# Output projections as stages of their own, a head-group loop turned by half, and gain work inside the FFN loop of a decoder layer

## Chip, core and metric

The kernel runs on one core of a Trainium2 chip. The metric is the device time of one execution in microseconds. TensorE is called PE in the rows, VectorE DVE, ScalarE ACT, GpSimd POOL, SyncE SP; SP issues nearly all DMAs.

## What is computed

One decoder layer for 256 tokens of width 2048 in float32. The part that matters, cut from the reference:

```python
mod = jax.nn.silu(c) @ w_ada[l] + b_ada[l]            # 2048 x 12288, six pieces of 2048
sh_m, sc_m, ga_m, sh_f, sc_f, ga_f = jnp.split(mod[:, None, :], N_MOD, axis=-1)
h = rmsnorm(x, g_pre_mix[l]) * (1.0 + sc_m) + sh_m
# token mixer, 16 heads of 128
hq, hf, hi, hg, cq, ckv, kr, gate_a, gate_b = jnp.split(h @ w_in, split_idx, axis=-1)
o = hgrn2_chunked(q, k, v, log_f)                     # gated recurrence per head
o = rmsnorm(o, g_hg_out) * jax.nn.silu(hg)
y_a = o.reshape(B, S, HG_VWIDTH) @ w_o_hg             # output projection 1, 2048 x 2048
att = causal_block_attention(q_full, k_full, v_m)     # latent attention per head
y_b = att.reshape(B, S, MLA_HEADS * V_DIM) @ w_o_mla  # output projection 2, 2048 x 2048
merged = jax.nn.sigmoid(gate_a) * y_a + jax.nn.sigmoid(gate_b) * y_b
y = merged @ w_out
x = x + ga_m * rmsnorm(y, g_post_mix[l])
h = rmsnorm(x, g_pre_ffn[l]) * (1.0 + sc_f) + sh_f
y = swiglu(h, w_gate_up[l], w_down[l])                # 2048 -> 5632 -> 2048
return x + ga_f * rmsnorm(y, g_post_ffn[l])
```

## The kernel before

**Chunks.** All weights come in chunks of 256 rows by 512 columns (512 KB), 600 in all, through a ring of 4 slots. SP loads a chunk into `raw` (`load`) once VectorE is done with the slot. ScalarE rounds it into `whi` (`high`, line 374) once TensorE is done with the slot's last chunk. VectorE subtracts, `wlo = raw - whi` (`low`, line 1001). TensorE does 12 matmuls with it (`multiply`, lines 707 to 709): 2 token tiles x 2 row blocks x 3 products of high and low halves. So each engine's program is one list of chunks, in the same order, with its other work written by hand between them. ScalarE and VectorE can be three chunks ahead of TensorE and no more: VectorE reaches chunk c while TensorE is near c - 3. Each projection of 512 columns adds up in one of two pairs of PSUM banks; the pair is free for the next but one when somebody has read it (`pair_free`). Four more banks, XA and XB, serve transposes, scores and sums.

**Stages.** Start (80 chunks): input norm, compressed queries and keys, the gates; then a loop over 4 groups of 4 heads with 56 chunks each; `w_out` (32); the FFN as a loop over 11 blocks of 512 (264).

**A group (c = 0 to 55).** Chunks 0 to 7: queries, keys, rotary queries (two chunks of half width), values of the attention; 8 to 23: forget gate and query of the recurrence, beside which the attention runs (scores at 11, softmax, sums at 19); 24 to 39: value and output gate of the recurrence, beside which it runs: logarithms and `k` on ScalarE, 8 scans on VectorE behind `low(27)` (line 1264), `q_ready` behind 29 (line 1269), then eight decay levels at `DECAY` = c 31, 32, 34, ... 41. For a level GpSimd forms differences (`differences`, lines 192, 193), ScalarE exponentials, VectorE two products (`decay`, lines 1283, 1284), TensorE scores (line 896), VectorE a masked merge (line 1297). TensorE does the self scores (line 882) and those of the first level behind chunk 29. The output gate is made at c = 42 and 43 (lines 1318, 1321), the sum over keys behind c = 41, the norm at c = 45 (lines 1326 to 1335). Chunks 40 to 47: the group's part of `w_o_mla`; 48 to 55: its part of `w_o_hg`, 2 chunks per 512 columns. Each of these 8 products of a group is multiplied by its gate (line 1352) and added to `merged` (line 1357) on VectorE. Behind the loop `merged` is transposed (`transpose_merged`) and split for `w_out`.

**Modulation.** `mod` is a product of one row, so VectorE does it: `ada_acc += slot * csilu` (line 1008), one operation per 512 KB load. The first 64 loads belong to the start; the others, 128, go at one per chunk at c = 3 to 18 and 24 to 39 of each group (`ada_chunk`), through two slots of `ada_raw`; SP issues a load when the operation two before is done. TensorE sums the partitions (`sum_rows`, line 742, 8 matmuls per sum). The gains behind the two post norms are spread over the partitions with diagonals (`make_gain`, `spread_gain`, lines 1365 and 927), both in the `w_out` stage.

A program-level float32 matmul of the small kind counts as two instructions in the trace; a transpose as one.

## Time and profile before

| | |
|---|---|
| median of 3 runs | 1981.98 us (1979.76 to 1985.1) |
| profiled execution | 1982.95 us, its span 1981.0 us |
| busy TensorE, VectorE, ScalarE, GpSimd | 1859.5, 1375.7, 885.5, 138.9 us |
| first, second, third, fourth group | 200.3, 206.6, 202.1, 203.7 us |
| `w_out` stage, FFN from its second chunks to the last block | 100.8, 714.0 us |
| DMA, mean | 213 GB/s |

A busy time counts instructions in execution; those of TensorE overlap their neighbours, so its waits are best seen as idle time in front of an instruction. The releaser named behind it is the last to come of those that it waited for. "issue" as a releaser means that the profile shows none. The granted clock is a share of the full one.

### The profile page before, as it was taken

Reading aid. Unit: us, or ns where it says so; the run is one execution under the profiler, and the core shown is the slowest. Engines: PE = TensorE matmul, PEld = TensorE weight load, DVE = VectorE, ACT = ScalarE, POOL = GpSimd, SP = SyncE. Lnnn points to the kernel's source line nnn. Section 1 sums busy time; section 2 is a strip of 40 time slices with the busy share of each in tenths; the row PEclk is TensorE's granted clock in tenths of the full one; section 3 lists DMA queues with packets and bytes.
Section 4 is the critical chain, followed back from the end, with each engine's and each line's share of the span. In section 5 each row is a group of like instructions: output and inputs, shape, how many; then the busy total and the mean of one; then the engine's idle time right before and its main releaser. Section 6 shows DMA issues by size and latency. Waiting matters only on the chain. (4 is left out here: it accounts for less than half of the span.)

```text
span 1981.0 us, 25357 instructions
## 1 busy us (share of the span) xinstructions
PE 1859.5 (94%) x8940; PEld 1554.0 (78%) x8940; DVE 1375.7 (69%) x1336; ACT 885.5 (45%) x985; POOL 138.9 (7%) x76
## 2 busy tenths in 40 slices
PE   1999999999899999899989996999999999999995
PEld 1877888788787878787878885788888888888884
DVE  5799767789769876987698755556555655565555
ACT  4544455643463436444644443444434444444442
POOL 0000000140014000500050000000000000000000
PEclk9999999999999999999999998999999999999998
DMA  9996648665776486748774653565556555555662
GB/s 380 360 352 233 195 158 305 233 205 168 280 233 224 155 292 230 237 133 291 248 244 140 212 174 98 185 193 189 190 191 190 190 190 191 191 190 187 194 191 75
DMA packets 116247, 421.78 MB, mean 213 GB/s; under 512 B 12976, under 2 KB 13232, under 8 KB 115888
## 3 DMA queue, kind: packets, MB, share of 16 engines
q1 hardware_dynamic: 116144, 420.47, 63.0%
q8 instruction: 56, 0.92, 0.2%
q14 instruction: 47, 0.39, 0.1%
HBM read 418.33 MB, written 2.10 MB: 212 GB/s over the span
## 5 line engine op out<-in xcount | busy, mean ns | idle before, releaser
L1001 DVE TENSOR_TENSOR wlo<-raw,whi 128x1024 fp32r<-128x1024 f32 (+1 forms) x600 | 731.2, 1222 | 421.6 <-ACT whi L374 408.4
L374 ACT ACTIVATE whi<-raw 128x1024 fp32r<-128x1024 f32 (+1 forms) x600 | 628.7, 1052 | 729.2 <-PE PS L709 666.1
L707 PE MATMUL PS<-whi,hT_hi 128*128 128x512 f32 x1664 | 663.7, 399 | 25.8 <-DVE wlo L1001 18.3
L708 PE MATMUL PS<-wlo,hT_hi 128*128 128x512 f32 x1664 | 652.7, 392 | 0.0
L709 PE MATMUL PS<-whi,hT_lo 128*128 128x512 f32 x1664 | 652.6, 392 | 0.0
L707 PEld LDWEIGHTS PS<-whi,hT_hi 128*128 128x128 f32 x1664 | 315.8, 190 | 96.3 <-DVE wlo L1001 16.7
L709 PEld LDWEIGHTS PS<-whi,hT_lo 128*128 128x128 f32 x1664 | 315.3, 189 | 67.5
L708 PEld LDWEIGHTS PS<-wlo,hT_hi 128*128 128x128 f32 x1664 | 316.0, 190 | 62.6
L1008 DVE SCALAR_TENSOR_TENSOR ada_acc<-ada_raw,csilu,ada_acc 128x1024 f32<-128x1024 f32 x133 | 196.6, 1478 | 42.7 <-DMA ada_raw<-in_ada 41.5
L707 PE MATMUL PS<-whi,oT_hi 128*128 128x512 f32 x480 | 188.1, 392 | 2.4 <-DVE oT_lo L1459 2.4
L708 PE MATMUL PS<-wlo,oT_hi 128*128 128x512 f32 x480 | 187.7, 391 | 0.0
L709 PE MATMUL PS<-whi,oT_lo 128*128 128x512 f32 x480 | 187.7, 391 | 0.0
L707 PEld LDWEIGHTS PS<-whi,oT_hi 128*128 128x128 f32 x480 | 90.8, 189 | 21.7 <-DVE oT_lo L1459 2.8
L708 PEld LDWEIGHTS PS<-wlo,oT_hi 128*128 128x128 f32 x480 | 90.8, 189 | 18.9
L709 PEld LDWEIGHTS PS<-whi,oT_lo 128*128 128x128 f32 x480 | 90.7, 189 | 18.9
L661 POOL TENSOR_TENSOR stat<-stat,con 128x2 f32<-128x2 f32 (+1 forms) x10 | 12.7, 1267 | 1244.4 <-DVE stat L1059 1215.3
L192 POOL TENSOR_TENSOR dec<-bT 128x512 f32<-128x512 f32 x28 | 56.8, 2029 | 580.2 <-DVE bT L1264 509.6
L1169 DVE TENSOR_TENSOR gate<-gate,PS 128x1024 f32<-128x1024 f32 x64 | 78.0, 1219 | 14.7 <-PE PS L709 14.6
L896 PEld LDWEIGHTS PS<-zT 128*128 128x128 f32 x448 | 58.4, 208 | 24.6 <-DVE zT L1284 23.5
L896 PE MATMUL PS<-zT 128*128 128x64 f32 x448 | 60.4, 292 | 17.9 <-DVE zT L1284 17.9
L555 ACT ACTIVATE dec<-dec 128x1024 f32<-128x1024 f32 (+1 forms) x32 | 32.2, 1007 | 82.2 <-POOL dec L193 79.5
L193 POOL TENSOR_TENSOR dec<-bT 128x512 f32<-128x512 f32 x28 | 55.6, 1986 | 0.0
(206 smaller groups left out, 1494.2 us busy)
## 6 DMA issues: line engine op xcount, KB each, us to landing
ada_raw<-in_ada SPq DMA_DIRECT2D x142, 512.0 KB, 4.7
raw<-in_w_gate SPq DMA_DIRECT2D x88, 512.0 KB, 4.2
raw<-in_w_up SPq DMA_DIRECT2D x88, 512.0 KB, 4.2
raw<-in_w_down SPq DMA_DIRECT2D x88, 512.0 KB, 4.2
raw<-in_w_start SPq DMA_DIRECT2D x80, 512.0 KB, 4.3
raw<-in_w_hf SPq DMA_DIRECT2D x32, 512.0 KB, 5.3
raw<-in_w_hq SPq DMA_DIRECT2D x32, 512.0 KB, 4.9
raw<-in_w_hi SPq DMA_DIRECT2D x32, 512.0 KB, 3.8
```

The lines of the kernel that those rows point to most:

```text
L192: eng.tensor_tensor(d[:, :, 1, :], b[:, :, 1, :], end, ALU.subtract)
L193: return eng.tensor_tensor(d[:, :, 0, :], end, b[:, :, 0, :], ALU.subtract)
L374: nc.scalar.activation(whi[:, pl.slot(c), 0:w], raw[:, pl.slot(c), 0:w], ACT.Copy)\
L555: nc.scalar.activation(dif, dif, ACT.Exp).then_inc(sig("decays"), 1)
L661: nc.gpsimd.tensor_tensor(src, src, con[:, K_POW:K_POW + width], ALU.pow)\
L707: nc.tensor.matmul(o, hi[:, kt, tok], whi[:, s, cols], start=start, stop=False)
L708: nc.tensor.matmul(o, hi[:, kt, tok], wlo[:, s, cols], start=False, stop=False)
L709: last = nc.tensor.matmul(o, lo[:, kt, tok], whi[:, s, cols], start=False, stop=stop)
L896: last = nc.tensor.matmul(PS[:, XA + L % 4, i * 64:(i + 1) * 64], z[:, i], zt[:, i, :, 1, :], start=True, stop=True)
L1001: nc.vector.tensor_tensor(wlo[:, s, 0:w], raw[:, s, 0:w], whi[:, s, 0:w].bitcast(F32), ALU.subtract)\
L1008: last = nc.vector.scalar_tensor_tensor(out=ada_acc[:], in0=slot, scalar=csilu[:, a:a + 1], in1=ada_acc[:], op0=ALU.mult, op1=ALU.add)
L1169: nc.vector.tensor_tensor(dst, dst, banks(2 * p), ALU.add).then_inc(pair_free[p], 1)
```

## The change

The two output projections leave the loop. The normalised attention and recurrence results of all heads are kept as rows (`att`, `mixed`), and behind the loop follow two stages of 32 chunks, `w_o_mla` then `w_o_hg`, each summed over all heads in PSUM. Their inputs are transposed from rows in 8 steps of two head tiles each (`transpose_rows(u)`, u = 0 to 7 for `att`, 8 to 15 for `mixed`, 16 to 23 for the merged result), split by `rows_high` and `rows_low`, and stored where older operands are done (`row_home`, `row_freed`). The gates are applied by `gated`.

The loop is turned: a lead (attention part of group 0), 3 turns of 40 chunks, and a tail. In a turn t = 0 to 15 are value and output gate of group i with its recurrence (t = c - 24), t = 16 to 39 the attention part of group i + 1 (t = c + 16), with the recurrence's last steps (sum at 17, gate 19, norm 21) beside it. VectorE runs the modulation in halves of 512 columns: two dependent operations per load, at the chunks `ADA_LEAD`, `ADA_TURN`, `ADA_OM`, `ADA_OH`. The last 32 loads (the piece `ga_f`) are taken 4 per turn of the FFN loop, in turns 1 to 8; turn 9 stands outside the loops and spreads the sum with 4 matmuls of 512 columns; the gain rows come from HBM.

```diff
-ADA_A = 2
+ADA_G = 3
+ADA_P = KD // 2
...
+        att = sb("att", [P, TT, D])
+        mixed = sb("mixed", [P, TT, D])
-        merged = sb("merged", [P, TT, D])
...
-        ADA_AT = [3, 3 * CD]
-        DECAY = [31 + 3 * L // 2 for L in range(len(LEVELS) + 1)]
+        ADA_LEAD = [21 + 2 * r for r in range(ADA_P)]
+        ADA_TURN = [4, 5, 9, 12, 15] + list(range(18, 18 + ADA_G * ADA_P - 5))
+        ADA_OM = [6, 8, 10, 13, 15, 17, 18, 20]
+        ADA_OH = [5, 7, 9, 12, 14, 17, 20, 22]
+        ADA_FF = [2, 8, 17, 21]
+        ADA_FF_LOAD = [0, 3, 6, 12]
+        DECAY = [7 + 3 * L // 2 for L in range(len(LEVELS) + 1)]
+        T_CROSS, T_SUM, T_OG, T_OSQ, T_ON = DECAY[-1] - 2, DECAY[-1], 19, 20, 21
...
+        def row_bank(u):
+            return XB + u % 2 if u < HALF else XA + u % 2 if u < KP else XA + u % 4
...
@@ SP
+                    if pl is place_oh and c == CD:
+                        sp.wait_ge(sig("rows_transposed"), KP)
+                        sp.dma_start(x2, x).then_inc(sig("x_again"), 16)
...
+                    if with_ada and c in ADA_FF_LOAD:
+                        sp.wait_ge(ada_step, n * 4 + (q + ADA0 + 2 * S_FF - 5))
+                        sp.dma_start(ada_raw[:, q % 2], ada2[n * 4 + (q - 4)]).then_inc(ada_loaded[q % 2], 16)
...
@@ ScalarE
+            for t in range(AHEAD, T_UQ):
+                high(place_tail, t)
+                recur(place_tail, t, NG - 1)
+                if t in (3, 4):
+                    rows_high(2 * t - 6)
+                    rows_high(2 * t - 5)
+            for c in range(N_ST):
+                high(place_om, c)
+                recur(place_tail, T_UQ + c, NG - 1)
+                for u in {2: (4, 5), 3: (6, 7), 11: (8, 9), 13: (10, 11), 28: (12,), 29: (13,), 30: (14,), 31: (15,)}.get(c, ()):
+                    rows_high(u)
...
@@ TensorE
+            def transpose_rows(u):
+                stage_i, kp = divmod(u, KP)
+                before = u - 2 if u < KP or u in (KP, KP + 1) else u - 4
+                if 0 <= before and u not in (HALF, HALF + 1, KP + 2, KP + 3):
+                    pe.wait_ge(sig("rows_low"), before + 1)
...
+            with pe.Fori(0, NG - 1) as i:
+                pl = place_turn(i)
+                for t in range(T_N):
+                    mix(pl, t)
+                    recur(pl, t, i)
+                    attention(pl, t, i + 1, i, ada_sum, i * (2 * ADA_G * ADA_P) + (ADA0 + 2 * ADA_P + 2 * ADA_G * ADA_P))
+            for t in range(T_UQ):
+                mix(place_tail, t)
+                if t in (0, 1):
+                    if t == 0:
+                        pe.wait_ge(sig("f_sigmoid"), NG)
+                    transpose_rows(2 * t)
+                    transpose_rows(2 * t + 1)
+                if t == DECAY[0] - 2:
+                    pe.wait_ge(sig("rows_low"), HALF)
+                recur(place_tail, t, NG - 1)
+            pe.wait_ge(sig("level5_merged"), NG)
+            transpose_rows(4)
+            transpose_rows(5)
+            for c in range(N_ST):
+                stage_step(0, place_om, c)
+                recur(place_tail, T_UQ + c, NG - 1)
+                for u in {0: (6, 7), 8: (8, 9), 10: (10, 11), 25: (12,), 26: (13,), 27: (14,), 28: (15,)}.get(c, ()):
+                    transpose_rows(u)
...
+                if with_gain:
+                    pe.wait_ge(ada_step, ADA0 + 2 * S_FF + 4 * FF_ADA)
+                    for j in range(GD):
+                        last = nc.tensor.matmul(PS[:, XA + j, :], ones, last_sum[:, j * NW:(j + 1) * NW], start=True, stop=True)
...
@@ VectorE
+            def ada_piece(r, loads, steps, acc):
+                a = r % ADA_P
+                dve.wait_ge(ada_loaded[r % 2], loads * 16)
+                for k in range(2):
+                    if a or k:
+                        dve.wait_ge(ada_step, steps + k)
+                    ada_accumulate(2 * a + k, ada_raw[:, r % 2, k * NW:(k + 1) * NW], acc)
...
+            for t in range(AHEAD, T_UQ):
+                low(place_tail, t)
+                recur(place_tail, t, NG - 1)
+                if t in (4, 5):
+                    rows_low(2 * t - 8)
+                    rows_low(2 * t - 7)
+            def gated(pl, which, n):
+                cols = start_sum[2 + which * GD + n]
+                nc.vector.tensor_tensor(cols, banks(2 * p), cols, ALU.mult).then_inc(pair_free[p], 1)
+                if which:
+                    nc.vector.tensor_tensor(start_sum[2 + n], start_sum[2 + n], cols, ALU.add).then_inc(sig("merges"), 1)
+            for c in range(N_ST + AHEAD):
+                low(place_om, c)
+                recur(place_tail, T_UQ + c, NG - 1)
+                for u in {3: (4, 5), 4: (6, 7), 12: (8, 9), 14: (10, 11), 29: (12,), 30: (13,), 31: (14,), 32: (15,)}.get(c, ()):
+                    rows_low(u)
...
+            with dve.Fori(1, FF_ADA + 1) as n:
+                channel(n, True)
+            channel(FF_ADA + 1, False, True)
+            with dve.Fori(FF_ADA + 2, NF) as n:
+                channel(n, False)
```

In a turn each engine handles a chunk, then the step of `recur` due at it, then that of `attention`, and VectorE a modulation load last.

## Rows read from the trace of the kernel before

**Rows 1.** Windows: stretch, length, busy of PE, PEld, DVE, ACT, POOL; PEclk, DMA
```profile
291.00:491.30 200.30, 192.56 (x1002) 162.16 (x1000) 164.22 (x160) 98.08 (x117) 30.65 (x16) 0.98 0.67 226
491.30:697.90 206.60, 194.50 (x1001) 163.76 (x1001) 164.29 (x160) 97.86 (x115) 31.63 (x16) 0.98 0.66 223
697.90:900.00 202.10, 193.74 (x1000) 163.39 (x1000) 162.32 (x159) 95.97 (x114) 31.64 (x16) 0.97 0.67 226
900.00:1103.70 203.70, 195.15 (x1011) 165.05 (x1012) 165.72 (x161) 97.67 (x116) 31.64 (x16) 0.97 0.68 229
1103.70:1204.50 100.80, 97.22 (x471) 81.22 (x469) 56.01 (x81) 46.34 (x60) 0.00 (x0) 1.00 0.58 192
...
1223.00:1937.00 714.00, 709.86 (x3185) 588.10 (x3184) 403.19 (x347) 294.12 (x284) 0.00 (x0) 1.00 0.58 187
```

**Rows 2.** Waits of the whole run: us in total, times, longest
```profile
PE PS L707 <- DVE wlo L1001: 23.5, 14, 5.9
...
PE PS L896 <- DVE zT L1284: 17.9, 10, 4.2
...
DVE wlo L1001 <- issue: 13.1, 3, 6.3
```

**Rows 3.** Timeline of TensorE, second group and FFN: start, length, [idle before]
```profile
596.47 2.05 PE L882 MATMUL PS<-qT,kT 128*128 128x128 f32 x16 [0.22 <-DVE qT L1269]
602.75 3.34 PE L896 MATMUL PS<-zT 128*128 128x64 f32 x16 [4.24 <-DVE zT L1284]
...
1659.91 0.39 PE L707 MATMUL PS<-whi,hT_hi 128*128 128x512 f32 x1
...
1662.63 0.39 PE L707 MATMUL PS<-whi,hT_hi 128*128 128x512 f32 x1
```

**Rows 4.** Windows again: three seams between groups; behind the first decay wait
```profile
491.30:521.30 30.00, 24.65 (x112) 19.74 (x113) 19.39 (x23) 12.22 (x13) 0.00 (x0) 0.94 0.73 258
697.90:727.90 30.00, 27.24 (x129) 22.32 (x130) 20.51 (x24) 12.35 (x15) 0.00 (x0) 0.94 0.83 283
900.00:930.00 30.00, 26.81 (x127) 22.05 (x128) 21.53 (x24) 12.88 (x14) 0.00 (x0) 0.94 0.83 282
603.10:610.00 6.90, 6.90 (x25) 6.03 (x25) 6.48 (x7) 1.06 (x1) 4.45 (x3) 0.51 0.82 302
```

**Rows 5.** Timeline of VectorE, around the first wait of Rows 3
```profile
583.12 1.23 DVE L1001 TENSOR_TENSOR wlo<-raw,whi 128x1024 fp32r<-128x1024 f32 x1 [3.72 <-ACT whi L374]
...
585.46 2.63 DVE L1264 TENSOR_TENSOR_SCAN bT<-con,bT 128x128 f32<-128x128 f32 x8
...
591.12 2.06 DVE L1001 TENSOR_TENSOR wlo<-raw,whi 128x1024 fp32r<-128x1024 f32 x1
...
595.13 1.21 DVE L1269 TENSOR_TENSOR qT<-qT,PS 128x1024 f32<-128x1024 f32 x1
...
602.01 0.69 DVE L1284 TENSOR_TENSOR zT<-kT,dec 128x512 f32<-128x512 f32 x1
```

**Rows 6.** Groups of the whole run: busy, mean ns of one
```profile
L742 PE MATMUL PS<-con,ada_acc 128*128 128x1 f32 x192 | 22.7, 248 | 0.8 <-ACT merged L410 0.8
```

**Rows 7.** Timeline of VectorE, end of the second group
```profile
651.88 1.23 DVE L1001 TENSOR_TENSOR wlo<-raw,whi 128x1024 fp32r<-128x1024 f32 x1 [4.03 <-ACT whi L374]
...
655.41 1.22 DVE L1001 TENSOR_TENSOR wlo<-raw,whi 128x1024 fp32r<-128x1024 f32 x1
...
660.08 1.21 DVE L1326 TENSOR_REDUCE stat<-dec 128x8 f32<-128x1024 f32 x1
...
665.65 1.22 DVE L1001 TENSOR_TENSOR wlo<-raw,whi 128x1024 fp32r<-128x1024 f32 x1
```

**Rows 8.** DMA issues of the page: KB each, us from issue to landing
```profile
ada_raw<-in_ada SPq DMA_DIRECT2D x142, 512.0 KB, 4.7
```

**Rows 9.** Timeline of ScalarE, two stretches of the second group
```profile
582.99 2.06 ACT L538 ACTIVATE kT<-kT,lb 128x256 f32<-128x256 f32 x4
...
649.88 1.03 ACT L381 ACTIVATE side<-PS 128x1024 f32<-128x1024 f32 x1
```

More of the change, by code:

```diff
@@ L339, in _, with load_turn, due @@
-            for c in range(GD * CD):
+            def load_turn(pl, t, back, front):
+                if t < T_UQ:
+                    load(pl, t, (w_hi, w_hg)[t // CD][back, t % CD])
+                elif t < T_HF:
+                    w = (w_uqn, w_uk, w_uqr, w_uv)[(t - T_UQ) // CL]
+                    load(pl, t, w[front, (t - T_UQ) % CL], NW // 2 if T_UR <= t < T_UV else NW)
+                else:
+                    load(pl, t, (w_hf, w_hq)[(t - T_HF) // CD][front, t % CD])
+            def due(steps, t, first):
+                return [r for r in range(len(steps)) if t == (steps[r - 2] + RING if r >= 2 else first + r)]
@@ new lines, in _ @@
+            for t in range(T_UQ, T_N):
+                load_turn(place_lead, t, None, 0)
+                for r in due(ADA_LEAD, t, T_UQ):
+                    load_ada(r, (r, r))
+            with sp.Fori(0, NG - 1) as i:
+                for t in range(T_N):
+                    load_turn(place_turn(i), t, i, i + 1)
+                    for r in due(ADA_TURN, t, 0):
+                        n = i * (ADA_G * ADA_P) + (ADA_P + r)
+                        load_ada(n, (n, r))
+            for t in range(T_UQ):
+                load_turn(place_tail, t, NG - 1, None)
@@ new lines, in _ @@
+            for pl, w, steps, first in ((place_om, w_omla, ADA_OM, S_OM), (place_oh, w_ohg, ADA_OH, S_OH)):
+                for c in range(N_ST):
+                    load(pl, c, w[c // CD, c % CD])
+                    for r in due(steps, c, 0):
+                        load_ada(first + r, (first + r, r))
+                    if pl is place_oh and c == CD:
+                        sp.wait_ge(sig("rows_transposed"), KP)
+                        sp.dma_start(x2, x).then_inc(sig("x_again"), 16)
@@ new lines, in width_of @@
+            def width_of(t):
+                return NW // 2 if T_UR <= t < T_UV else NW
+            for t in range(T_UQ + AHEAD, T_N + AHEAD):
+                high(place_lead, t, width_of(t))
+                attention(place_lead, t, 0, None)
+            with act.Fori(0, NG - 1) as i:
+                pl = place_turn(i)
+                for t in range(AHEAD, T_N + AHEAD):
+                    high(pl, t, width_of(t))
+                    recur(pl, t, i)
+                    attention(pl, t, i + 1, i)
@@ new lines, in _ @@
+            for c in range(AHEAD, N_ST + AHEAD):
+                low(place_oh, c)
+                if c == AHEAD:
+                    gated(place_om, 0, GD - 1) if GD * CD + 3 > N_ST + AHEAD - 1 else None
+                for u in {16: (16, 17), 24: (18, 19), 32: (20, 21)}.get(c, ()):
+                    rows_low(u)
+                if c in ADA_OH:
+                    r = ADA_OH.index(c)
+                    ada_piece(r, ADA_LOADS + (S_OH + r) // 2 + 1, ADA0 + 2 * (S_OH + r), ada_sum[0])
+                if c == 27:
+                    piece((NG - 1) * ADA_G * HPG + 2 * HPG, HPG, XA + 1, NG + 1)
+                if c > 3 and c % CD == 3:
+                    gated(place_oh, 1, c // CD - 1)
```

909 lines of the change are left out of this document (472 added, 437 removed).

## The prediction

> **What bounds the kernel now.** I read the windows by stage first. TensorE (PE) is busy in nearly all of each: 192.6 of 200.3 us in the first head group, 194.5 of 206.6 in the second, 709.9 of 714.0 in the FFN [rows 1]. VectorE (DVE) follows with 164 of some 203 us in a group. So only what makes TensorE wait, or run slowly, can be won. Its waits [rows 2] are for VectorE alone where the change reaches: 23.5 us for the low halves of weights, 17.9 us for decayed keys and queries.
>
> A weight chunk (512 KB, 12 matmuls) holds TensorE 2.72 us: the matmul that opens a chunk starts at 1659.91 and again at 1662.63 [rows 3]. Small matmuls go at about 0.115 us (16 in 2.05, the last one's own length off). A group has 54 chunks, 2 of half width, and some 1001 - 672 = 329 small ones: 147 + 3 + 38 = 188 us of work. The four groups take 200.3, 206.6, 202.1 and 203.7 us [rows 1], so some 61 us are lost in the loop. That is the pool. It has three parts:
> - The recurrence, per group: a wait of 4.2 us ahead of the first decay level [rows 3], one of 1.1 for the low half of the chunk before (it ends at 593.2 [rows 5], TensorE would be there at 592.0), some 1.3 in small ones: about 6.7.
> - The seams between groups: 5.4, 2.8 and 3.2 us of idle TensorE in their first 30 us [rows 4], 11.4 in all.
> - The clock. In the 6.9 us behind the 4.2 us wait the granted clock is 0.51, the level of 1.2 GHz instead of 2.4; in a seam it is 0.94 over 30 us, so 3.6 us at that level [rows 4]. Half of such a stretch is lost: 3.4 us per recurrence, 1.8 per seam, 19 in all.
>
> **The change, part by part.** *Operations.* The merges were 64 multiplies and adds in the loop, of the size of a weight's low half, 1.2 us [rows 5]. 8 multiplies and 4 adds are left: 52 x 1.2 = 62 us leave VectorE, off the path but for the seams. On TensorE the same 600 chunks and 96 head transposes stay. The sums over the modulation were 192 small matmuls [rows 6], of which 128 in this loop; 96 are left: 32 x 0.115 = -3.6 us. The spread of the second gain (32) becomes 8 of 512 columns. No fp32 one of that width is in the trace: at the pace of the wide fp32r ones (2.72 / 12) it is 1.8 us, at four times a small one 3.7; I take 3.7, since the small ones are fp32 too, which cancels what goes. Sum -3.6, or -5.5.
>
> *The recurrence, now at chunks t = 0 to 17 of a turn* (t = c - 24), keeps its distances, but of 16 modulation operations beside it 5 pairs of half width stay, none at t = 3, 6 and 7. I shift the old times of VectorE [rows 5]. The scans follow the low half of t = 3 (583.1 to 584.3) at once and end at 586.9 instead of 588.1. GpSimd's differences start then, and beside them an SBUF operation takes 2.06 instead of 1.22, as at 591.12. Low of t = 4: 588.9. A modulation pair at t = 4: 591.3. Low of t = 5: 593.3, as before, so the wait of 1.1 stays, 1.3. The product with the query, 1.2, now goes ahead of the modulation pair: 594.5, pair 596.0, two lows 598.3, the two decay products 599.6 instead of 602.7. TensorE does chunk 5 from 593.3 and the self scores to 597.9: it waits 1.7 instead of 4.2. With the small ones 3.5 instead of 6.7.
> Two things eat into it. VectorE's jump back to the head of the loop is an idle time of 13.1 us in three, the longest 6.3 [rows 2], at the seams; now it lies just ahead of the scans. It had 3.7 us of idle there [rows 5] and 1.3 of a modulation operation, so the first jump costs some 2.4, the second nothing. Three recurrences in the loop: 20.5 before, 3 x 3.5 + 2.4 = 12.9 after: **-7.6**. Bounds: 0 (all eaten by jumps and GpSimd) and -14 (both waits go).
> The Trainium skill (Runtime: NRT & Kernel Launch, Instruction fetch mechanics) says that a taken branch to code outside the window of two pages must fetch it first. The trace agrees: the short FFN loop shows no such wait. If the new body fitted, the sum would be 2.4 lower; it has about as many operations, so I don't count on it.
>
> *The seam, now t = 18 to 29.* The merges are gone from it, but normalisation, rotation and a modulation pair at every chunk come together. From the old times [rows 7]: low of t = 19 ends at 653.0, gate 655.4, pair 656.8 (a pair is two dependent half operations: I take 1.4, between 1.2 for one whole and 2.1 beside GpSimd), low and pair of t = 20 (half width) 658.8, low 659.4, normalisation as from 660.08 to 665.65, 5.6: 665.0, pair 666.4, low of t = 22 at 667.5. TensorE gets there at 665.3 (sum over keys done at 656.1, as before, then two chunks of 2.72, two of half width and the 0.9 us of a group's transposes): wait 2.3. Then pair, low, rotation (six operations on 256 elements, 2.1), pair, low of t = 24 at 674.8; TensorE has done two chunks by 673.0: wait 1.8. Behind it TensorE has the scores (5.4 us of small matmuls) and VectorE catches up. A modulation load needs 4.7 us [rows 8] from the release of its buffer; pair to pair leaves 3.7 to 4.0, so up to 1 us a chunk is lost to it in t = 24 to 29, covered by the scores. 4.1 us each, 3 x 4.1 = 12.3 instead of 11.4: **+0.9**. Bounds -11 and +15 (pairs of 2.1).
>
> *The tail.* After the loop the last recurrence stands alone, with new transposes and their waits. Behind t = 1 TensorE waits for the low half of attention rows 0 and 1, which VectorE makes at t = 4, since its bank is to be reused; queued behind that wait is the query transpose, on which ScalarE and all the recurrence hang. ScalarE copies the rows only after the keys (582.99 to 585.0) [rows 9] and a weight copy; VectorE then ends scans at 586.9, a slowed low at 589.2, two row halves at 590.4. Then four row transposes and the eight of the query, 1.4 us: TensorE, due at 585.5 past them (chunk 1 ends at 583.8), is there at 591.8: **+6.3**. Queued behind it on TensorE are all chunks; ScalarE's sigmoid of the query and the decay levels wait for it. The old waits of this recurrence vanish in it: **-6.4**. The same again in the first chunk of the stage behind it: rows 6 and 7 wait for the low half of rows 4 and 5, which VectorE makes only at its chunk 3, behind the gate. Scalar's sigmoid ends at 650.9 [rows 9], two row copies and a weight 653.1, low 654.2, gate 656.6, row halves 657.8; TensorE is due past both at 652.2, is there at 658.3: **+6.0**. Bounds for both together 0 (rows early) and +15.
>
> *Stages.* In the two new stages VectorE has some 65 us of work in 87 us and every other row transpose is asked for chunks later: 0. The output stage has 3.6 us of idle TensorE (100.8 - 97.2) [rows 1]; I give half of it to its start, where eight transposes follow each other and wait for their split, which the change spreads out: **-1.8**. Loading x again (2 MB) moves a stage ahead, under ring slack as before: 0.
>
> *FFN.* 4 modulation operations of 1.3 us per turn: VectorE from 403 in 714 us [rows 1], 37 in 66, to 42 in 66. SP, whose queue holds the weights too, waits at a modulation load for an operation at most one chunk off. Hidden, 0; without cover up to 5 us.
>
> *Clock.* Waits of 3 us in two parts resemble a seam, so 3 recurrences and 3 seams at 1.8 and two tail waits at 3.4: 17.6 instead of 19: **-1.4**. Bounds -9 and +5.
>
> Sum: -3.6 - 7.6 + 0.9 + 6.3 - 6.4 + 6.0 - 1.8 - 1.4 = -7.6. The profiled execution took 1982.95 us (span 1981.0 and 1.95 around it): 1975.4. The median of the runs is 1.0 lower: **1974.4**.
>
> **Rivals.** *Relief goes further (20%).* The loop's two recurrence waits go (3 x 3.0), their clock drops too (3 x 1.7), and the tail waits are halved (-6): 1974 - 20 = 1954; 1948 to 1964. For it: 62 us less on VectorE. Against it: its chain there was timed by ScalarE and GpSimd, which keep their work.
> *Waits only move (15%).* Jumps and GpSimd take the -7.6: 1982; 1980 to 1988. For it: TensorE's work is the same.
> *VectorE becomes the bound at the seam (19%): slower.* Place: t = 18 to 29, where a turn has 40 chunks instead of 56 for the same side work. Price: if a pair costs 2.1, seven pairs cost 4.9 more, with no slack at t = 22, and late loads some 4: 9 per turn, 27 in all, and 5 of clock: 2006. It decides once a seam costs about 4.5 us more than my 4.1; then over 1988.
> That the change doesn't do what it says, the gain rows or FFN pieces breaking into the FFN loop's rhythm, is worth 5 us at most and lies within these.
>
> **How the numbers follow.** Forecast 46%: 1966 to 1980. A measurement tells 0.3%, about 6 us, from no change, so the forecast splits at 1976: 30 below, 16 above. Faster by more: 0.30 + 0.20 = 0.50; within: 0.16 + 0.15 = 0.31; slower: 0.19. For 8 in 10 the range leaves out the lowest part of the first rival and the upper part of the third: 1955 to 1992.
>
> **What would show it.** Right: three waits of about 1.7 us ahead of the first decay level; waits of about 2 us at the chunks of the value and forget projections; one of about 6 ahead of the last query transpose, one of about 6 in the first chunk of the attention stage; FFN turns still at 66.2 us (24 chunks, 8 transposes); half clock in stretches of 3.4 us in the loop. Wrong: a loop turn of over 162 us, or a longer FFN turn. The largest risk is that all times on VectorE were carried over from one group.

## The result, and the profile after

The changed kernel takes 1955.68 us (median; 1952.78 to 1956.87), the kernel before 1981.14 beside it: a ratio of 0.9866 [0.9848, 0.9884], 25 us or 1.3% faster. The forecast was 1974.4, in a range of 1955 to 1992. The direction was right and the range just holds the time, but the size was not: the gain is more than three times the 7.6 us of the sum.

The profiled execution spans 1953.7 us, against 1981.0 before. Windows by stage, in the columns of [rows 1]; they are the three turns of the loop, the tail, the attention, recurrence and output stages:

```profile
291.10:441.70 150.60, 148.79 (x810) 127.91 (x810) 104.56 (x127) 83.40 (x103) 23.75 (x15) 1.00 0.57 196
441.70:592.40 150.70, 146.52 (x793) 125.55 (x792) 115.41 (x143) 78.70 (x97) 25.80 (x17) 0.98 0.64 224
...
742.90:830.00 87.10, 78.96 (x423) 67.28 (x422) 63.26 (x81) 45.52 (x63) 6.46 (x5) 0.95 0.68 234
830.00:917.50 87.50, 81.93 (x436) 70.62 (x435) 53.38 (x60) 40.48 (x44) 18.91 (x12) 0.95 0.37 124
917.50:1004.70 87.20, 87.20 (x405) 72.44 (x405) 58.91 (x63) 36.39 (x39) 0.00 (x0) 1.00 0.73 260
1004.70:1104.00 99.30, 99.30 (x464) 82.84 (x464) 67.95 (x82) 40.82 (x45) 0.00 (x0) 1.00 0.68 241
```

In a turn TensorE is idle for 2 to 4 us of some 150.6; in a group of the kernel before it was 7.7 to 12.1 of some 203 [rows 1]. The tail and the attention stage have 8.1 and 5.6 us of idle time (87.10 - 78.96, 87.50 - 81.93); behind them there is none up to 1104. The waits of the whole run say who was late:

```profile
PE PS L797 <- DVE wlo L1140: 14.7, 7, 5.9
PE PS L815 <- DVE cT_lo L1352: 5.8, 1, 5.8
PE PS L815 <- DVE hT_lo L1352: 5.6, 1, 5.6
PE PS L939 <- DVE zT L1416: 3.7, 3, 1.3
```

The first and the last answer to [rows 2]: 23.5 and 17.9 us have become 14.7 and 3.7. The two between are new, one each in the tail and in the first chunk of the attention stage, where the prediction had put 6.3 and 6.0. The wait that VectorE had for nothing but "issue", 13.1 us in three, is gone.

All that follows uses one measure: the time that TensorE **lost** in a stretch, from the first matmul of each chunk to that of the next, less its work there (0.227 us for a matmul of 512 columns, 0.112 for a small one, 0.43 for an fp32 one of 512, all at full clock). Idle time and half clock are both in it. ("Small" and "fp32" count records of the trace, two for each such matmul of the program.) In us, from one profiled execution each; a reading changes by 1.6 from one turn to another, as shown below, so differences of 1 to 2 us between two such readings say little:

| | three recurrences | three seams | attention chunks | last recurrence and 16 chunks, or tail and attention stage | first chunks and output stage |
|---|---|---|---|---|---|
| before | 31.4 | 16.0 | 5.4 | 11.9 | 19.5 |
| changed | 10.6 | 13.5 | 2.6 | 17.0 | 17.1 |

Recurrence: chunks 24 to 39 of a group, t = 0 to 15 of a turn. Seam: the last 16 chunks and the first 8, or t = 16 to 23. "16 chunks" are the last of the fourth group, with the wait at their end for the transposed input of `w_out`. "First chunks" are the first 8 behind the start. The differences sum to -23.4 (the FFN and the start differ by 0.1). With 64 small matmuls less and 8 wide ones more (-7.2 + 3.4) that is -27.2; the spans differ by 27.3.

### The profile page after: what moved, and what is told of

It reads as the page before. It is cut to its first block, busy times and chain, and to the rows that moved or that the text cites. A ratio compares the mean times of both kernels' runs of the same rounds, so it can differ in the third digit from the quotient of the medians.

```text
span 1953.7 us, 24693 instructions
## 1 busy us (share of the span) xinstructions
PE 1846.4 (95%) x8884; PEld 1548.0 (79%) x8884; DVE 1314.4 (67%) x1375; ACT 885.0 (45%) x991; POOL 109.9 (6%) x75
## 4 chain that ended last, share of the span: by engine, by line
issue 61%; PE 30%; POOL 4%; DVE 3%; ACT 1%; DMA 1%; SPq 0%; POOLq 0%; DVEq 0%; ACTq 0%
PE PS L797 9%; PE PS L799 9%; PE PS L798 9%; POOL dec L194 2%; DVE ada_acc L1147 1%; POOL dec L195 1%; PE PS L815 1%; DMA zT<-in_ada 1%; DVE wlo L1140 1%; PE PS L939 1%; PE PS L832 1%; PE PS L857 0%; POOL dec L190 0%; ACT whi L449 0%; POOL stat L752 0%
## 5 line engine op out<-in xcount | busy, mean ns | idle before, releaser
L1140 DVE TENSOR_TENSOR wlo<-raw,whi 128x1024 fp32r<-128x1024 f32 x600 | 731.5, 1222 | 464.3 <-ACT whi L449 463.9
L449 ACT ACTIVATE whi<-raw 128x1024 fp32r<-128x1024 f32 x600 | 629.8, 1053 | 758.8 <-PE PS L799 686.9
L797 PE MATMUL PS<-whi,cT_hi 128*128 128x512 f32 (+1 forms) x608 | 239.2, 393 | 9.5 <-DVE wlo L1140 7.1
L799 PE MATMUL PS<-whi,cT_lo 128*128 128x512 f32 (+1 forms) x608 | 236.8, 390 | 0.0
L798 PE MATMUL PS<-wlo,cT_hi 128*128 128x512 f32 (+1 forms) x608 | 236.8, 389 | 0.0
L797 PEld LDWEIGHTS PS<-whi,cT_hi 128*128 128x128 f32 x608 | 116.8, 192 | 33.4 <-DVE wlo L1140 7.8
L799 PEld LDWEIGHTS PS<-whi,cT_lo 128*128 128x128 f32 x608 | 116.3, 191 | 23.5
L798 PEld LDWEIGHTS PS<-wlo,cT_hi 128*128 128x128 f32 x608 | 116.7, 192 | 22.8
L1147 DVE SCALAR_TENSOR_TENSOR ada_acc<-ada_raw,csilu,ada_acc 128x512 f32<-128x512 f32 (+1 forms) x148 | 119.7, 809 | 11.4 <-DMA ada_raw<-in_ada 8.1
L1309 DVE TENSOR_TENSOR gate<-gate,PS 128x1024 f32<-128x1024 f32 x64 | 78.0, 1219 | 14.7 <-PE PS L799 14.6
L194 POOL TENSOR_TENSOR dec<-bT 128x512 f32<-128x512 f32 x28 | 51.5, 1840 | 439.8 <-DVE bT L1397 365.2
```

The lines of the kernel that those rows point to most:

```text
L194: eng.tensor_tensor(d[:, :, 1, :], b[:, :, 1, :], end, ALU.subtract)
L449: nc.scalar.activation(whi[:, pl.slot(c), 0:w], raw[:, pl.slot(c), 0:w], ACT.Copy)\
L797: nc.tensor.matmul(o, hi[:, kt, tok], whi[:, s, cols], start=start, stop=False)
L798: nc.tensor.matmul(o, hi[:, kt, tok], wlo[:, s, cols], start=False, stop=False)
L799: last = nc.tensor.matmul(o, lo[:, kt, tok], whi[:, s, cols], start=False, stop=stop)
L1140: nc.vector.tensor_tensor(wlo[:, s, 0:w], raw[:, s, 0:w], whi[:, s, 0:w].bitcast(F32), ALU.subtract)\
```

## Experiments

They set out from two theories. That of the prediction: VectorE has less work beside the recurrence, and its jump stays and moves. Its rival: the seams were relieved too, by the merges' going or by something about the jump, and the new pairs at t = 18 to 29 took part of that back.

A time is followed by its ratio to the kernel before, run beside it, with the 95% interval. Runs whose computation is cut leave out part of the result; they tell times alone.

**Merges small.** In the kernel before, the multiply is cut to one column, as is the add behind it:

```diff
-nc.vector.tensor_tensor(scaled[n % 2], banks(2 * p), start_sum[2 + n], ALU.mult)
+nc.vector.tensor_tensor(scaled[n % 2][:, :, 0:1], banks(2 * p)[:, :, 0:1], start_sum[2 + n][:, :, 0:1], ALU.mult)
```

> The kernel before, with the 64 operations of the merges cut to one column per row each (they keep their place, their waits and their signals; most of the merge isn't computed). Some 62 us leave VectorE, all of it between the recurrence and the head of the next group; the number of instructions in VectorE's loop stays. Theory A, the merges' own time makes the seams' idle: the 11.4 us of idle TensorE at the three seams fall to about 5, with some half clock behind them: 7 to 9 us faster in all, near 1973. Theory B, VectorE's idle of 4 to 7 us at its jump back makes it: the jumps stay, as do the seams; 0 to 2 us faster. The recurrence's wait of 4.2 us stays under both.

1973.04 us, 0.9954 [0.9937, 0.9971]: 7.7 us faster. The seams lost 12.1 us instead of 16.0, the attention chunks 0.8 instead of 5.4, the recurrences 31.2. The size is theory A's, but the seams still lost 12 us, and VectorE's jumps still took 5.0, 5.3 and 4.5 us: part of B holds too.

**Modulation thin.** In the kernel before, 11 operations a group on two columns:

```diff
-ada_chunk(g, d * KD + a)
+ada_chunk(g, d * KD + a, d == 1 and a not in (4, 5, 9, 12, 15))   # True: columns 0:2 alone
```

> The kernel before, with 11 of the 16 modulation operations that lie beside the recurrence in each group cut to two columns (those left at full width are at chunks 28, 29, 33, 36 and 39, where the changed kernel has its five pairs; most of one modulation sum isn't computed). Theory A, the modulation operations are what made VectorE late for the first decay level: the wait of 4.2 us falls to 1.5 or less and the one of 1.1 goes, 3 to 4 us per recurrence, with clock 12 to 18 us faster over four. Theory B, the chain there is timed by GpSimd's differences and ScalarE's exponentials, and the changed kernel gained by something else: less than 1 us per recurrence, 0 to 4 us faster. The forecast in the prediction lies between (some 2.5 per recurrence).

1966.66 us, 0.9922 [0.9903, 0.994]: 14.1 us faster. The three recurrences lost 17.2 us instead of 31.4, 4.7 less each: theory A. The changed kernel lost only 10.6 there, with the same operations left, so something is still missing.

**Both.** The two edits together.

> The kernel before with both cuts of the two runs beside it (merges to one column, 11 modulation operations per group to two). If they act at different places, their gains add, 15 to 26 us under theory A of both, and VectorE's work is then close to that of the changed kernel while its loop keeps its 321 instructions and its jumps: what the changed kernel gained beyond this run is the jump's and the order's. If one cause hides behind the other, the gain exceeds the sum.

1959.98 us, 0.9893 [0.9875, 0.9911]: 20.8 us faster, where 7.7 and 14.1 sum to 21.8: the gains add.

**Long body.** In the changed kernel, waits for one early signal, 8 at each of 13 chunks (t = 30 to 42, where the loop ends; the expectation says 15). The 104 waits make 52 instructions:

```diff
 low(pl, t, width_of(t))
+if 30 <= t < 45:
+    for _ in range(8):
+        dve.wait_ge(sig("masks_loaded"), 16)
```

> The changed kernel with 52 instructions more in VectorE's loop over the groups, each a wait for a signal that came long ago (21 ns each in the trace of the changed kernel, so 1.1 us a turn on VectorE, spread over 15 chunks): its body has 331 instructions instead of 279, where the kernel before had 321. Theory A, the idle at the jump goes with the length of the body: 4 to 7 us of idle at VectorE's two jumps back return (they were 0.3 us in the changed kernel); VectorE then starts the scans late, and TensorE waits 1 to 4 us more in each of the two recurrences behind a jump, 2 to 8 us slower than the changed kernel, near 1960. Rival, the idle had to do with what VectorE had in flight or with its waits: the jumps stay at 0.3 us and the time stays within 2 us.

1956.84 us, 0.9872 [0.9854, 0.9891]: as the changed kernel, and the jumps stay at 0.3 us with a body of 331 instructions. Theory A falls: the kernel before paid with 321. The rival put forward in its stead (what VectorE has in flight) was tested next.

**Code moved.** The kernel before with 63 instructions ahead of everything on VectorE:

```diff
+for _ in range(128):
     dve.wait_ge(sig("vectors_loaded"), 16)
```

> The kernel before with 63 instructions more ahead of everything on VectorE, each a wait for a signal that has come (1.3 us in all, where VectorE is idle at the start). Nothing of the loop changes but the place of its code. The long body with 52 waits more paid nothing at its jump (0.32 us with 331 instructions, against 4.0 to 7.3 us with 321 in the kernel before), so length alone isn't it. Theory A, it is where the body lies against the pieces in which code is fetched: moved on by 63 instructions the 321 fit, VectorE's three jumps fall to 0.3 us, the seams lose some of their 11.4 us of idle TensorE: 4 to 9 us faster. Rival, the idle at the jump belongs to the content of the loop or to the wait behind it: jumps of 4 to 7 us stay, time unchanged.

1966.91 us, 0.9933 [0.9916, 0.995]: some 13 to 15 us faster (by the ratio and by the times) without a change in the loop. The same place on VectorE's timeline, where the first group ends (start, length, [idle before]), first of the kernel before, then of this one:

```profile
492.50 1.23 DVE L1357 TENSOR_TENSOR merged<-merged,zT 128x1024 f32<-128x1024 f32 x1
499.98 1.23 DVE L1001 TENSOR_TENSOR wlo<-raw,whi 128x1024 fp32r<-128x1024 f32 x1 [6.26 <-issue]
```

```profile
491.46 1.23 DVE L1358 TENSOR_TENSOR merged<-merged,zT 128x1024 f32<-128x1024 f32 x1
492.60 1.22 DVE L1001 TENSOR_TENSOR wlo<-raw,whi 128x1024 fp32r<-128x1024 f32 x1
```

The three seams lost 4.9 us instead of 16.0, the attention chunks 0.8 instead of 5.4, the recurrences 31.4 as ever. What is at work stands in the page's third part, at the queue that loads instructions. In order: the kernel before, this one, and the next experiment, which moves SyncE's code too:

```profile
q14 instruction: 47, 0.39, 0.1%
```

```profile
q14 instruction: 32, 0.26, 0.1%
```

```profile
q14 instruction: 17, 0.14, 0.0%
```

15 packets go with VectorE's three jumps and 15 with SyncE's: each jump loaded its code again. The Trainium skill (Runtime: NRT & Kernel Launch, Instruction fetch mechanics) says that code comes in pages of 256 instructions, that two are held, and that a taken branch to a page outside them waits for it. The runs agree, and add what decides here: a body of 321 or 331 instructions may or may not pay, by where it begins. Counted in VectorE's trace, the loop's body is instructions 308 to 628 in the kernel before and 559 to 889 in the moved long body below, which both pay; 371 to 691 in this run, 370 to 700 in the long body and 370 to 648 in the changed kernel, which don't. Pages of 256 fit all five, a slow body touching three pages and a fast one two, if the trace begins 142 to 203 instructions into a page. That offset is inferred and no run varied it by itself, so the boundary of a page is argued, not shown.

**SyncE's code moved too** (64 instructions more, right ahead of its loop).

```diff
+for _ in range(128):
+    sp.wait_ge(sig("trunk_mean"), 1)
 with sp.Fori(0, NG) as g:
```

> The kernel before with VectorE's code moved on by 63 instructions, as in the run of that name, and also SyncE's loop over the groups moved on by 64 (waits for a signal that has come, right ahead of its loop). SyncE's body has 310 instructions, and its jumps took 4.3 to 4.5 us in the kernel before and also where VectorE's code was moved. Theory A, place of the code: SyncE's jumps fall to 0.3 us too, and since the ring of four chunks covers 4.4 us of late issue, the time stays within 2 us of 1966.9. Rival, the late loads are what is left of the seams: 3 to 6 us faster still.

1965.31 us, 0.9921 [0.9907, 0.9934]. Its jumps fell to 0.3 us and the time by 1.6, or 2.4 by the ratios, whose intervals overlap with those of the run before. That is near the first theory's 2 us: the weight ring hides most of SyncE's 4.4 us, while VectorE's jumps cost 13 to 15. The changed kernel has SyncE's jumps at 0.3 us too (238 instructions).

**Long body moved.** The changed kernel with the long body and 189 instructions ahead, to bring the jump back.

```diff
-dve.wait_ge(sig("vectors_loaded"), 16)
+for _ in range(380):
+    dve.wait_ge(sig("vectors_loaded"), 16)
```

> The changed kernel with the body of 331 instructions and, ahead of everything on VectorE, 189 waits for a signal that has come (4 us at the start, where VectorE is idle). Theory A (place of the code): moved on by 189 instructions the body fits no longer, and the two jumps back take 4 to 7 us instead of 0.3. They stand ahead of the scans: TensorE then waits 2 to 4 us more in each of the two recurrences behind them, 3 to 9 us slower than the long body unmoved (1956.8). This is the price that the prediction put at 2.4 us for the first jump and nothing for the second. Rival: no jump idle, time as the long body.

1969.1 us, 0.9938 [0.9923, 0.9953]. The jumps are back, at 2.8 us, and q14 has 36 packets instead of 24. But none of the 12 us can be seen to be theirs. The recurrences lost 10.7 us (10.6 in the changed kernel) and the seams 13.5 (13.5), and what is late is the start. It shows in one wait of TensorE, in the long body first and then in this run:

```profile
PE PS L815 <- ACT gate L481: 34.7, 1, 34.7
```

```profile
PE PS L815 <- ACT gate L481: 48.1, 1, 48.1
```

189 such waits kept VectorE for 19 us (its first operation begins at 22.2 instead of 3.2), 0.1 us each and not 0.02, and it isn't idle there after all. So one half of the experiment stands: a jump of 2.8 us ahead of the scans costs nothing, since VectorE is idle for 4.9 us there (the first row of the timeline of VectorE in the section on the prediction).

**Both, and code moved.** Merges small, modulation thin and VectorE's code moved.

> The kernel before with merges cut to one column, 11 modulation operations per group cut to two columns, and the 63 instructions ahead that take VectorE's jumps down to 0.3 us. Known: the two cuts give 20.8 us, the moved code 14.7. Theory A, the jump and the work on VectorE are late for the same matmul at the head of a group, so that taking the jump away covers what the merges cost: the gains overlap, 1951 to 1956 (merges' 7.7 us within the jump's). Rival, they add: 1981.6 - 20.8 - 14.7 = 1946.

1945.01 us, 0.9817 [0.9803, 0.9831]: 36.9 us faster. The rival was nearer, everything adds: 20.8 + 14.7 = 35.5. The seams lost 0.9 us, the recurrences 19.6.

**Loads gone too.** In addition, the loads of the 11 thin operations are left out, which then read a resident tile:

```diff
 def load_ada(g, a):
+    if a >= KD and a - KD not in (4, 5, 9, 12, 15):
+        return
```

> The kernel before with merges and 11 modulation operations per group cut, VectorE's code moved on by 63 instructions, and the loads of those 11 operations left out too (512 KB each; the cut operations read two columns of a resident tile instead, so most of one modulation sum isn't computed). In the run without this last step VectorE still waited 55 us for modulation loads in the four groups, 46 times, among them just before and between its decay products; the changed kernel 18 us. That run lost 5.7 to 7.0 us per recurrence, the changed kernel 2.5 to 4.1 (time of TensorE beyond its work). Theory A, VectorE's waits for loads that can be asked for only when the operation before has freed the buffer are the part of the recurrence that is still open: 3 us per recurrence go, 12 in all, 1933. Rival, GpSimd's differences and ScalarE's exponentials time the levels: within 3 us of 1945.

1936.78 us, 0.9778 [0.9762, 0.9795]: 7.7 us faster by the ratios (0.0039 of 1980), where theory A said 12. The recurrences lost 4.4 us each instead of 6.5, nearly all of the difference at chunk 29, the one ahead of the first decay level. One thing more changed in this run: without those loads SyncE's body has 266 instructions instead of 310, and its jumps fell from 4.3 to 0.3 us. By the run on SyncE's code that is worth up to some 2 us of the 7.7, but hardly in the recurrences, which lost 30.1 us there instead of 31.4. VectorE's timeline from the first decay products to the second, with thin operations and their loads ("Modulation thin", which has full merges and unmoved code), then without loads:

```profile
588.16 0.69 DVE L1284 TENSOR_TENSOR zT<-qT,dec 128x512 f32<-128x512 f32 x1
...
592.94 0.22 DVE L1009 SCALAR_TENSOR_TENSOR ada_acc<-ada_raw,csilu,ada_acc 128x2 f32<-128x2 f32 x1 [2.35 <-DMA ada_raw<-in_ada]
...
595.14 0.67 DVE L1284 TENSOR_TENSOR zT<-qT,dec 128x512 f32<-128x512 f32 x1
```

```profile
581.95 0.68 DVE L1291 TENSOR_TENSOR zT<-qT,dec 128x512 f32<-128x512 f32 x1
...
587.33 0.68 DVE L1291 TENSOR_TENSOR zT<-qT,dec 128x512 f32<-128x512 f32 x1
```

An operation of 0.22 us waits 2.35 us for a load that could be asked for only when the one before had freed its buffer; the level behind it comes 7.0 us after the first instead of 5.4 (6.8 to 7.3 in the run that differs by the loads alone). VectorE's waits for modulation loads in the four groups fell only from 55.3 to 39.7 us: most of them stand where nothing is late for them.

**Halves.** As the last, with the five operations that stay cut in two halves.

```diff
+for j in range(2):
+    nc.vector.scalar_tensor_tensor(out=acc[:, j * NW:(j + 1) * NW], in0=slot[:, j * NW:(j + 1) * NW], ...)
```

> As the run without the loads, with the five modulation operations per group that stay beside the recurrence cut into two halves of 512 columns each, as they are in the changed kernel. There GpSimd's second difference took 1.22 us beside a pair of halves, and 2.02 beside a whole operation in the kernel before. Theory A, halves let GpSimd through, and the first decay products come 1 us earlier in each recurrence: 3 to 5 us faster than the run with whole operations. Rival, what one gains the other loses: within 1 us, or slower by the 0.3 us that a pair takes longer than a whole operation alone.

1943.15 us, 0.9805 [0.9785, 0.9824]: 5 to 6 us slower. The product with the query comes 10.7 us behind the start of the scans instead of 9.7, and the recurrences lost 6.5 us each instead of 4.4. Theory A had the sign wrong. Here halves cost 2.1 us a recurrence, and by this run they are a cost of the change too. Whether the order pays for them is tested next.

**Pair first.** The changed kernel with the pair at t = 5 ahead of the product.

```diff
-recur(pl, t, i)
+if t != 5:
+    recur(pl, t, i)
 ...
+if t == 5:
+    recur(pl, t, i)      # behind ada_piece
```

> The changed kernel with one exchange on VectorE in each turn of the loop: at t = 5 the modulation pair goes ahead of the product with the query (as it stood before the change). The pair is 1.45 us. Theory A, the decay products behind the query's product are what the first level waits for, so each of the three recurrences (two in turns that show it fully) waits 1.4 us longer: 3 to 5 us slower than the changed kernel, with clock up to 8. Rival, the exponentials of ScalarE end later than the product, and the pair fits into that: within 1 us.

1957.67 us, 0.9878 [0.9863, 0.9894], the recurrences 11.5 us instead of 10.6. The product comes 2.2 us later (10.6 instead of 8.4), the decay products only 0.8 (14.6 instead of 13.8), because the pair had stood in that same stretch anyway. By the ratios this is 2.4 us slower, and 0.8 us a turn fits it: between the two, neither theory's figure. The reading of 11.5 hides it, since this execution had one stretch of half clock less, 1.6 us.

**Later row transposes.** The changed kernel, rows 2 and 3 behind chunk 3 of the tail and rows 6 and 7 behind chunk 1 of the attention stage. On TensorE (ScalarE's copies of rows 2 and 3 move from t = 4 to 5, of 6 and 7 from c = 3 to 4):

```diff
-if t in (0, 1):
+if t in (0, 3):
...
-for u in {0: (6, 7), 8: (8, 9), ...
+for u in {1: (6, 7), 8: (8, 9), ...
```

> The changed kernel with two of its row transposes later: rows 2 and 3 of the attention result behind chunk 3 of the tail instead of chunk 1 (and so behind the query transpose), rows 6 and 7 behind chunk 1 of the attention stage instead of chunk 0; ScalarE's copies and VectorE's differences follow. Theory A, the two waits of 5.8 and 5.6 us come from a bank that is asked for again too soon, and nothing else is late there: both go, and with them the half clock behind them (two stretches of 6.8 us): 12 to 18 us faster than the changed kernel, 1938 to 1944. Rival, VectorE is late there anyway and the waits move to the self scores of the tail and to the low halves of the weights: 0 to 6 us faster.

1939.39 us, 0.9786 [0.9769, 0.9802]: 16.3 us faster than the changed kernel. Both waits are gone (0.2 us are left of one) and tail and stage lost 1.4 us instead of 17.0. Theory A holds, in the upper part of its range.

**Pairs off the seam, 1.** The changed kernel with no pair at t = 20, 21, 35 and 36, and four more at t = 10, 13, 16 and 17 beside the recurrence (the six of the expectation count those at 18 and 19, which were there before):

```diff
-ADA_TURN = [4, 5, 9, 12, 15] + list(range(18, 18 + ADA_G * ADA_P - 5))
+ADA_TURN = [4, 5, 9, 10, 12, 13, 15, 16, 17, 18, 19, 22, 23, 24, 25, 26, 27, 28, 29, 30, 31, 32, 33, 34]
```

> The changed kernel with its modulation pieces set otherwise within a turn: none at chunks 18 + 2 and 18 + 3 (t = 20 and 21, ahead of the one wait of 2.5 us in each turn), t = 22 and 23 kept, and six more beside the recurrence (t = 10, 13, 16, 17 and 18, 19 as before), the last at t = 34 instead of 36. Theory A, VectorE is late at t = 22 by the pairs ahead of it: 2.9 us less work there, the three waits of 2.5 us go, with clock 8 to 12 us faster. Rival, they come back as waits at the decay levels beside which the new pairs stand, or at t = 19: within 3 us of the changed kernel, to either side.

1955.83 us, 0.9869 [0.9853, 0.9886]: no change. The seams lost 9.0 us instead of 13.5, the recurrences 13.5 instead of 10.6, the attention chunks 5.0 instead of 2.6. The rival holds, and at the recurrences the loss is where it put it.

**Pairs off the seam, 2.** With the later row transposes; only t = 17 is added beside the recurrence, and t = 37 behind.

```diff
+ADA_TURN = [4, 5, 9, 12, 15, 17, 18, 19, 22, 23, 24, 25, 26, 27, 28, 29, 30, 31, 32, 33, 34, 35, 36, 37]
```

> The kernel with the later row transposes (1939.4), with the pairs at t = 20 and 21 moved to t = 17 and 37 and nothing added to the decay levels but the one at 17. Moving six pairs beside the recurrence cost as much as the emptied seam gave (1955.8 against 1955.7). Theory A, the three waits of 2.5 us at t = 22 go and no new ones come: 4 to 8 us faster, 1931 to 1936. Rival, with pairs taken away the load of the next chunk's low half is what t = 22 waits for, or the levels pay again: within 2 us of 1939.4.

1932.76 us, 0.9749 [0.9736, 0.9762]: 6.6 us faster than with the later transposes alone, 23 us faster than the changed kernel. The seams lost 8.1 us. Theory A holds on the time, though its "three waits go" doesn't in full: 2.7 us are still lost at each seam. It is the fastest kernel of the study.

## Why the prediction was right or wrong

In the measure of lost time, the prediction's terms (its half clock put to the place where it had it) stand beside what was measured. The 1.8 us that the kernel before lost at the end of its fourth group are counted here as the start of the output stage, where the prediction has them:

| term | predicted | measured |
|---|---|---|
| operations | -3.6 | -3.8 |
| three recurrences | -7.6, clock -4.8: -12.4 | -20.8 |
| three seams | +0.9 | -2.5 |
| attention chunks | 0 | -2.8 |
| tail and attention stage | +5.9, clock +3.4: +9.3 | +6.9 |
| output stage, start | -1.8 | -1.8 |
| first chunks, rest of the output stage | 0 | -2.4 |
| FFN | 0 | 0 |
| sum | -7.6 | -27.2 |

- **The step that failed most: the recurrences, -12.4 where -20.8 came.** The kernel before was read nearly right (30.7 us lost in three by the prediction's terms, 31.4 measured). After the change the prediction left 18.3 and the runs show 10.6. Of the 7.7 between, 2.4 are the jump that didn't come, 2.0 the clock, and the rest, 3.3, the waits: 0.57 us instead of 1.3 ahead of chunk 5, 1.24 instead of 1.7 ahead of the first level, in each turn. (3 times its own 6.7 is 20.1, not the 20.5 that it took off; the slip is 0.4.)
- **Operations: right.** A record of the gain's wide fp32 matmul took 0.43 us, the eight records of its four matmuls 3.4 us; I had taken 3.7.
- **The chain ahead of the first decay level: right in kind, up to 0.9 us too late.** Here is the recurrence of the second turn on VectorE, then TensorE's wait for it, and the stretch behind it in the columns of [rows 1]:

```profile
520.56 1.23 DVE L1140 TENSOR_TENSOR wlo<-raw,whi 128x1024 fp32r<-128x1024 f32 x1 [4.91 <-ACT whi L449]
521.70 2.63 DVE L1397 TENSOR_TENSOR_SCAN bT<-con,bT 128x128 f32<-128x128 f32 x8
...
530.05 1.21 DVE L1401 TENSOR_TENSOR qT<-qT,PS 128x1024 f32<-128x1024 f32 x1
...
535.50 0.69 DVE L1416 TENSOR_TENSOR zT<-kT,dec 128x512 f32<-128x512 f32 x1
...
539.89 0.68 DVE L1416 TENSOR_TENSOR zT<-kT,dec 128x512 f32<-128x512 f32 x1
```

```profile
536.24 2.00 PE L939 MATMUL PS<-zT 128*128 128x64 f32 x16 [1.24 <-DVE zT L1416]
```

```profile
538.20:541.60 3.40, 3.40 (x10) 2.62 (x10) 3.27 (x5) 1.06 (x1) 2.03 (x3) 0.50 0.66 239
```

  TensorE's wait there was 1.2 us where I had 1.7, and 4.2 before [rows 3]. The granted clock fell to half for 3.4 us behind it, where it had been 6.9 us before [rows 4]. Behind the same waits it didn't fall in the first turn, which lost 2.5 us; the other two lost 4.0. So 1.6 us of a recurrence come or not, from one turn to another.
- **"With the small ones 3.5 instead of 6.7": what is behind it.** I followed the chain to the first level and priced VectorE's operations, not its waits for the loads that they bring. It waited for modulation loads 40.8 us in the four groups before, a row that I hadn't read, and 17.6 in the changed kernel:

```profile
DVE ada_acc L1008 <- DMA ada_raw<-in_ada: 40.8, 33, 3.7
```

  The second level comes 4.4 us behind the first (535.50 to 539.89 above), and came 6.4 to 7.4 behind it before. TensorE, though, waited little at the levels behind the first: 0.3 to 0.6 us once or twice a group before, not at all now, about 1 us of lost time per recurrence. Of the 6.9 us that each recurrence gained, the runs show 4.7 for the operations' time and 2.1 for their loads, but also 2.1 of cost for halves. The order ahead of the first level gives back 0.8. So some 1.4 us per recurrence have no run of their own; the order at the later levels wasn't tested.
- **"Now it lies just ahead of the scans ... the first jump costs some 2.4": the second step that failed.** I had cited the rule on pages and didn't count on it, since the new body has about as many operations. It has 279 instructions where it had 321, and jumps in 0.3 us. Those 2.4 us never came, and a jump of 2.8 us at the new place cost nothing either. In the sum the miss is no more than that. As an account of the kernel before it is larger: the sum had the three jumps of [rows 2] (13.1 us of "issue") inside the seams' idle and gave them no price of their own, and taking them away alone gives 13 to 15 us, as much as half of what the change gained. In the changed kernel the pairs at the seam take most of it back.
- **The seams: near in size, by luck.** I had +0.9 from two waits of 2.3 and 1.8 us that take the place of the old ones. Of the two one came, 2.4 us at t = 22:

```profile
598.64 0.50 PE L797 MATMUL PS<-whi,cT_hi 128*128 128x512 f32 x1 [2.38 <-DVE wlo L1140]
```

  The one at t = 24 didn't: TensorE ran at half clock behind the first wait, 3.4 us of it in each seam, and so came later. Beneath that the change did much more than I saw, both ways. Without jump, merges and dense modulation the three seams lose 0.9 us instead of 16.0; the changed kernel loses 12.6 more than that. I put this down to its pairs, since moving two of seven took 5.4 away again; that the other five make the rest wasn't tested.
- **The tail: right in mechanism and size.** 5.8 and 5.6 us for 6.3 and 6.0, for the reason given: taking the reason away took the waits away, 16.3 us with the clock behind them. With clock I had 19.1 us lost there in place of 9.8; it was 17.0 in place of 10.1.
- **Output stage and FFN: right.** The wait at the start of the output stage in the kernel before is gone, with 1.8 us lost around it:

```profile
1106.04 0.50 PE L707 MATMUL PS<-whi,hT_hi 128*128 128x512 f32 x1 [1.59 <-DVE hT_lo L1372]
```

  FFN turns take 66.2 us in both kernels (69.6 in the one turn that has the gain's wide matmuls).
- **First chunks: left out.** The first group of the kernel before had a wait of 1.6 us for a low half at chunk 8, behind three modulation operations. The lead of the changed kernel has its first modulation load at chunk 21, and that wait is gone: 2.1 us that I hadn't priced.
- **Attention chunks: left out.** They lost 5.4 us before, and 0.8 once the jump or the merges were gone: what was late in the seam had been handed on. The changed kernel lost 2.6.

The causes found don't quite make up the whole. From the kernel before: jumps, merges and modulation operations -36.9 (measured together), tail +16.3 (taken away alone), operations -3.8, output stage and first chunks -4.2, loads -7.7, halves +5 to 6, and +12.6 at the seams, which is a difference between two traces and no run. That is some -18, against -25 by the times and -27.3 by the spans. So 7 to 9 us of the gain stay open; the order ahead of the first level, 2.4 by its run, is part of them.

The rivals: "Relief goes further" came nearest (1948 to 1964, measured 1955.7). It had the right place, the recurrence, but its halved tail didn't come, and it didn't name the jump. That the time falls into it is in part luck. "VectorE becomes the bound at the seam" was there as a force, up to 12.6 us of its 27, and was outweighed.

## What to carry to other kernels

Read every line of "issue" waits at a loop's end and price it where it falls. A jump that waits for its code could here be removed by some dozens of instructions ahead of the loop, and cost nothing visible where its engine was idle anyway. When operations are moved off a chain, price the waits for the loads that they bring, and not their time alone; but count only those waits that stand on the chain. Where a bank is asked for twice in a row behind a slow round over three engines, ask for it a chunk or two later: here two such places were worth 16 us. When causes are added up, put in those with the other sign too.

## What the runs showed of the hardware

- VectorE's jump back in a loop took 0.3 us or 4.0 to 7.3 us for one and the same body of 321 instructions, by where its code began; 0.3 or 2.8 us for one of 331. SyncE's took 0.3 or 3.9 to 4.5 us for 310. The queue that loads instructions showed 5 packets more for each slow one of the 321 and of the 310. For the 331 it showed 12 more for two slow ones and the 189 added instructions together.
- A wait for a signal that has long come, in a row of 63 or 189 of them, took 0.1 us each.
- At full clock a record of an fp32 matmul with 512 columns took 0.43 us, and there are two records for each such matmul (eight for four); an fp32r one, with one record, took 0.227.
- GpSimd's differences on 512 columns took 1.03 us beside an idle VectorE and up to 2.19, by what ran on VectorE:

```profile
526.33 1.22 POOL L195 TENSOR_TENSOR dec<-bT 128x512 f32<-128x512 f32 x1
527.51 1.53 POOL L194 TENSOR_TENSOR dec<-bT 128x512 f32<-128x512 f32 x1
529.00 2.02 POOL L195 TENSOR_TENSOR dec<-bT 128x512 f32<-128x512 f32 x1
```

  The first ran beside halves of modulation operations (1.29 and 1.41 us). The second ran beside the end of a half and the start of a low half of full width, which took 2.10, the last beside the rest of it and the start of the product with the query.
